# Second FFN: one subtraction per chunk of four k-tiles in place of two

## The chip, the cores and the metric

The kernel runs on one core of a Trainium2 chip. The metric is the device time of one execution in microseconds (us), the lower the better. The five engines of the core run their own instruction streams and wait for each other through semaphores: TensorE (PE in the profile, its weight loads PEld), VectorE (DVE), ScalarE (ACT), GpSimd (POOL) and SyncE (SP), which here issues the DMAs.

## The reference

One macaron layer on 256 tokens of width 2048 in float32: an FFN, a mixer of windowed attention and mLSTM, and a second FFN, each behind an RMS norm that is modulated by a condition, then a last norm. The change is in the second FFN alone:

```python
def _swiglu(x, w_in, w_out):
    a, b = jnp.split(x @ w_in, 2, axis=-1)
    return (jax.nn.silu(a) * b) @ w_out
...
u = _modulate(_rmsnorm(h, norm3_g[l]), sh3, sc3)
h = h + 0.5 * gt3 * _swiglu(u, ffn2_w_in[l], ffn2_w_out[l])
return _rmsnorm(h, final_g)
```

`w_in` is 2048 x 11264 and `w_out` 5632 x 2048.

## The kernel before

**Numbers in two parts.** TensorE multiplies in a rounded float32 format (fp32r). To keep float32's accuracy each operand is split into a rounded value `hi` and a rest `lo` = value - `hi`, and each product is three matmuls: activations' `hi` by weights' `hi` (line 862), activations' `lo` by weights' `hi` (line 866), activations' `hi` by weights' `lo` (line 870).

**Weights.** They come from memory in chunks of four k-tiles: `raw`, 128 partitions x 4 x 512 values, 1 MB, in a ring of four. A chunk is worked on in two halves, called units (`half` 0 and 1, two k-tiles each). ScalarE casts a unit's weights into `hi` (line 1445), a ring of four units, so of two chunks. VectorE subtracts and writes `lo` (line 2051 in `split`), a ring of four chunks. TensorE then does the 12 matmuls of the unit. Three semaphores count units: `hi_done` (casts), `lo_done` (rests), `unit_used` (TensorE is through). ScalarE's cast of a unit waits until TensorE is through with the unit four before it; TensorE waits for `hi_done` ahead of its first matmul of a unit and for `lo_done` ahead of the last four, those on line 870.

**The second FFN.** Its hidden width is cut into three parts of 4, 4 and 3 groups of 512 columns (`PARTS`); the phases are `ffn2_in0`, `ffn2_out0`, `ffn2_in1`, and so on. In ten groups, listed in `JOBS`, a block of 2 x 128 tokens x 4 k-tiles x 2 x 512 columns is multiplied with seven block products in place of eight (B11, T1, T2, T3, B21, T4, B22). They are the four groups of `ffn2_in1`, two groups of `ffn2_out1` (of two column blocks each), the three of `ffn2_in2` and the first of `ffn2_out2`. For them VectorE forms sums of weight blocks in float32 (`fast_sum`, lines 2296 to 2305), ScalarE casts them (line 1511), and VectorE takes their rests (`fast_rest`, line 2315). The other chunks of such a group are plain ones, 6 in nine of the groups and 4 in the last, so 12 or 8 units. They are listed by `fast_plain`, and called unit 0 to unit 11 here.

**The order on VectorE.** It is written out by hand in `fast_body` of the vector block. In a loop over the plain units it does the unit's rest, and behind certain units other work. Behind unit 3 come the rests of the last three block products and the seed of `pb`. Behind unit 5 of a part's last input group come sums of activation operands (`s_sums`), and behind unit 8 their rest (`s_rest`). Behind unit 7 comes `nat_evac`, the two rests of the hidden values of the group before (line 2280). Behind unit 9 of an output group comes `add_out` (lines 2512 and 2517). And for the next group's block products: two sums behind unit 7, one behind unit 8, one behind unit 9, and one rest behind each of units 8 to 11.

The order on TensorE is: products and units 0 and 1 interleaved, unit 2, product B22, then units 3 to 11 one behind the other. ScalarE casts a unit, then does its own side work behind the same units.

Of the kernel before, what the change touches and what calls it, by code (L numbers as in the profile page):

```python
# [26 lines left out]
F32 = mybir.dt.float32  # L27
F32R = mybir.dt.float32r
I32 = mybir.dt.int32
ALU = mybir.AluOpType  # L30
# [31 lines left out]
def build(nc, x, c, positions, w_ada, b_ada, norm1_g, ffn1_w_in, ffn1_w_out, norm2_g, w_in,  # L62
# [116 lines left out]
    def s_used(q, n):  # L179

        on_dve = sum(kt not in ON_PE[x // KD] for x in range(KD * q + n) for kt in (x % KD,))
        return on_dve, KD * q + n - on_dve
# [32 lines left out]
    with ExitStack() as ctx:  # L215
        def sb(name, shape, dt=F32):
            return ctx.enter_context(nc.sbuf_tensor(name, shape, dt))
# [4 lines left out]
        def sem(name):  # L222
            return ctx.enter_context(nc.semaphore(name))
# [11 lines left out]
        hi = sb("hi", [P, RING, 2, NC], F32R)  # L235
# [134 lines left out]
        hi_done = sem("hi_done")  # L370
        lo_done = sem("lo_done")
# [131 lines left out]
        def at_seam(ph, i, j):  # L503

            return i == 0 and j == 0 and any(ph is plan[name] for name in BEHIND)

        def slot_of(ph, i, j):

            return 0 if at_seam(ph, i, j - 1) else (ph.at(i) + j) % RING

        def raw_of(ph, i, j):

            return seam_raw[:, :, :] if at_seam(ph, i, j) else raw[:, slot_of(ph, i, j), :, :]

        def lo_of(ph, i, j):

            return seam_lo[:, :, :] if at_seam(ph, i, j) else lo[:, slot_of(ph, i, j), :, :]
# [6 lines left out]
        def hi_of(ph, i, j, half):  # L524

            if spare(ph, i, j):
                if j == 1:
                    return (hid_hi, hid_lo)[half][:, 12:16, :].rearrange("p (a k) t -> p a (k t)", a=2)
                k = 2 * (j - 2) + half
                return hi_a[:, :, :] if k == 3 else hi_b[:, k, :, :]  # L530
            return hi[:, (2 * (ph.at(i) + j) + half) % 4, :, :]
# [15 lines left out]
        def fast_plain(name, i):  # L547

            if name[5] == "i":
                return [(i, j, half, 4 + 4 * (j % 3) + 2 * half) for j in range(6) for half in (0, 1)]  # L550
            return [(b, j, half, 4 + 4 * j + 2 * half) for b in (2 * i, 2 * i + 1) for j in range(plan[name].per[b])
                    for half in (0, 1)]
# [1485 lines left out]
        def _(dve):  # L2038
# [8 lines left out]
            def split(ph, i, j, half, n, w=NC):  # L2047
                u = 2 * (ph.at(i) + j) + half
                dve.wait_ge(hi_done, u + 1)
                s = slice(2 * half, 2 * half + n)  # L2050
                dve.tensor_tensor(lo_of(ph, i, j)[:, s, 0:w], raw_of(ph, i, j)[:, s, 0:w],  # L2051
                                  hi_of(ph, i, j, half)[:, 0:n, 0:w].bitcast(F32), ALU.subtract)\
                    .then_inc(lo_done, 1)

            def start_tiles(q, kts):

                for kt in kts:
                    if kt in ON_PE[q]:
                        continue
                    k = 8 * q + kt // 2  # L2060
                    dve.wait_ge(ada_s_in[2 * (k % S_RING) + kt % 2], 16 * (k // S_RING + 1))
                    wt = ada_s[:, k % S_RING, kt % 2, :]
                    acc = ada_acc[:, q % 2, :]
                    if kt == 0:
                        if q > 1:

                            dve.wait_ge(flushed, q - 1)
                        dve.tensor_scalar(acc, wt, cond[:, 0:1], None, ALU.mult).then_inc(s_dve, 1)
                        continue
                    dve.wait_ge(s_dve, s_used(q, kt)[0])  # L2070
                    dve.scalar_tensor_tensor(out=acc, in0=wt, scalar=cond[:, kt:kt + 1], in1=acc,
                                             op0=ALU.mult, op1=ALU.add).then_inc(s_dve, 1)
# [197 lines left out]
            def turn_square(nb):  # L2270

                dve.wait_ge(nat_ok, nb + 1)
                dve.transpose(squared(nb), buf_b[:, :, :]).then_inc(nat_sq, 1)
# [9 lines left out]
            def hidden(ph, i):  # L2283

                dve.wait_ge(unit_used, 2 * (ph.at(i + 1)))
                dve.wait_ge(pa_free, ph.a0 + i + 1)
                dve.tensor_tensor(buf_b[:, :, :], buf_a[:, :, :], pb[:, :, :], ALU.mult)\
                    .then_inc(nat_ok, 1)
# [65 lines left out]
            def fast_body(name, i, mid=None, nat_last=0, hid_tail=None, gate=2):  # L2354

                ph, f = plan[name], FAST[name, i]
                inner = name[5] == "i"
                plain = fast_plain(name, i)
                last = len(plain)
                for n_, (b, j, half, k0) in enumerate(plain):  # L2360
                    split(ph, b, j, half, 2)
                    if n_ == 3:
                        if inner and i > 0:
                            hidden(ph, i - 1)
                            turn_square(ph.nat0 + i - 1)
                        elif inner:
                            mid(3)
                        elif i > 0:
                            add_out(ph, 2 * i - 1, gate)
                        elif name == "ffn2_out1":  # L2370
                            hid_tail()
                            turn_square(nat_last)
                        else:
                            hid_tail()
                            last_square(nat_last)
                        fast_rest(f, B21)
                        if name == "ffn2_out2":
                            last_blocks(PARTS[2] - 1, (0, 1))
                        fast_rest(f, T4)
                        if name == "ffn2_out2":  # L2380
                            last_blocks(PARTS[2] - 1, (2, 3))
                        fast_rest(f, B22)
                        fast_seed(f)
                        if name == "ffn2_out2":
                            nat_evac(nat_last, PARTS[2] - 1)
                    if name == "ffn2_out1" and i == 0 and n_ == 4:
                        nat_evac(nat_last, PARTS[1] - 1)
                    if inner and i > 0 and n_ == 7:
                        nat_evac(ph.nat0 + i - 1, i - 1)
                    if inner and i == ph.n - 1 and n_ == 5:  # L2390
                        s_sums(name.replace("in", "out"))
                    if inner and i == ph.n - 1 and n_ == 8:
                        s_rest(name.replace("in", "out"))
                    if not inner and n_ == last // 2 + 3:
                        add_out(ph, 2 * i, gate)
                        if name == "ffn2_out2":
                            times_final(0, None)
                    if f + 1 < len(JOBS):
                        if n_ == last - 5:
                            fast_sum(f + 1, T3)  # L2400
                            fast_sum(f + 1, T1)
                        if n_ == last - 4:
                            fast_sum(f + 1, T2)
                        if n_ == last - 3:
                            fast_sum(f + 1, T4)
                        if n_ >= last - 4:
                            fast_rest(f + 1, n_ - last + 4)
# [33 lines left out]
            def first_body(ph):  # L2441
# [17 lines left out]
                lo_unit(1)  # L2459
                start_lo(1)  # L2460
                start_tiles(1, (0,))
                lo_unit(2)
                start_tiles(1, (1,))
# [42 lines left out]
            def add_out(ph, b, gate):  # L2506

                bank, free = (pa, pa_free) if b % 2 == 0 else (pb, pb_free)
                dve.wait_ge(unit_used, 2 * (ph.at(b + 1)))
                gate_ready(gate, b)  # L2510
                row = gt_row[:, b * NC:(b + 1) * NC].unsqueeze(1).broadcast_to([P, TT, NC])
                dve.scalar_tensor_tensor(out=buf_a[:, :, :], in0=bank[:, :, :], scalar=1.0 if gate == 1 else 0.5,
                                         in1=row, op0=ALU.mult, op1=ALU.mult).then_inc(free, 1)
                use = (ph.a0 if b % 2 == 0 else ph.b0) + b // 2 + 1
                dve.wait_ge(free, use)
                hs = h[:, :, b * NC:(b + 1) * NC]
                dve.tensor_tensor(hs, hs, buf_a[:, :, :], ALU.add).then_inc(h_ok, 1)
# [282 lines left out]
            ph = plan["proj"]  # L2800
# [241 lines left out]
            ph = plan["up"]  # L3042
# [38 lines left out]
            ph = plan["ffn2_out2"]  # L3081
# [34 lines left out]
```

## Time and profile before

| | us |
|---|---|
| median of 3 runs (2061.7 to 2062.15) | 2061.86 |
| the profiled execution, its own time | 2061.43 |
| its span, first to last instruction | 2059.7 |
| TensorE busy in the span | 2037.7 (99%) |
| VectorE busy | 1716.6 (83%) |
| ScalarE busy | 1144.7 (56%) |

The mean granted TensorE clock is 0.999 of full speed. The chain of work that ended last is 96% TensorE, 2% DMA and 1% VectorE. The ten groups with seven block products stand between 1606 and 2017 us of the span, one group about every 42.3 us. Within them a 128x512 matmul starts every 0.227 us, so a unit of 12 takes 2.72 us.

### The profile page before, as it was taken

To read this page: it belongs to the slowest core of one execution; us is meant where nothing else is said; L and a number is where in the kernel's file an instruction comes from. 1 tells how busy PE (TensorE), PEld (TensorE's weight loads), DVE (VectorE), ACT (ScalarE), POOL (GpSimd) and SP (SyncE) were. 2 spreads that over 40 slices of the span, in tenths; PEclk is the share of its full clock that TensorE was granted. 3 is DMA by queue.
4 is the path that set the end of the run, shared out by engine and by line. 5 is a ranking of instruction groups with operands and counts; after the bars stand their busy time and mean duration, and the time that the engine had idled before them with its cause. 6 is when DMAs were issued, how large, how long until landed. Compare 5 with 4: busy or idle time off the path is not lost.

```text
span 2059.7 us, 24190 instructions
## 1 busy us (share of the span) xinstructions
PE 2037.7 (99%) x9235; PEld 1681.2 (82%) x9235; DVE 1716.6 (83%) x2069; ACT 1144.7 (56%) x1568; POOL 4.5 (0%) x22
## 2 busy tenths in 40 slices
PE   7999999999999999999999999999999999999998
PEld 6888888888888888888777888888888888888887
DVE  6998998888789889888877898979978677787786
ACT  4677444565345565446544676554444577755764
POOL 0000000000000000000000000000000000000000
PEclk9999999999999999999999999999999999999999
DMA  9998998998899778985555687568875655665554
GB/s 370 387 387 320 327 333 320 341 335 295 295 343 331 265 258 324 329 284 179 169 164 164 224 291 282 204 216 313 288 257 193 202 186 194 214 202 191 179 199 148
DMA packets 249571, 540.79 MB, mean 263 GB/s; under 512 B 11888, under 2 KB 14320, under 8 KB 248688
## 3 DMA queue, kind: packets, MB, share of 16 engines
q1 hardware_dynamic: 248368, 539.11, 74.3%
q8 instruction: 73, 1.20, 0.2%
q14 instruction: 42, 0.34, 0.0%
q10 hardware_dynamic: 1088, 0.15, 0.0%
HBM read 537.10 MB, written 2.11 MB: 262 GB/s over the span
## 4 chain that ended last, share of the span: by engine, by line
PE 96%; DMA 2%; DVE 1%; SPq 0%; issue 0%; ACT 0%; DVEq 0%
PE pa L862 14%; PE pb L862 14%; PE pa L870 14%; PE pb L870 14%; PE pb L866 13%; PE pa L866 13%; DMA raw<-in_ffn_w_in_dram 1%; PE pa L1015 1%; PE pa L1009 1%; PE pa L1012 1%; PE pa L1179 1%; PE pb L1170 1%; PE pb L1175 1%; PE pb L1179 1%; PE pa L1170 1%; PE pa L1175 1%
## 5 line engine op out<-in xcount | busy, mean ns | idle before, releaser
L1445 ACT CAST hi<-raw 128x1024 fp32r<-128x1024 f32 (+2 forms) x682 | 702.4, 1036 | 768.5 <-PE pb L870 355.1
L2051 DVE TENSOR_TENSOR lo<-raw,hi 128x1024 fp32r<-128x1024 f32 (+2 forms) x682 | 809.1, 1200 | 267.5 <-ACT hi L1445 264.5
L2150 DVE SCALAR_TENSOR_TENSOR ada_acc<-ada_w,cond,ada_acc 128x1024 f32<-128x1024 f32 (+1 forms) x240 | 275.0, 1146 | 6.6 <-DVE ada_acc L2150 0.5
L862 PE MATMUL pa<-hi,act_hi 128*128 128x512 f32 x840 | 231.9, 394 | 0.0
L862 PE MATMUL pb<-hi,act_hi 128*128 128x512 f32 x840 | 227.7, 393 | 0.0
L870 PE MATMUL pb<-lo,act_hi 128*128 128x512 f32 x840 | 224.6, 389 | 0.0
L870 PE MATMUL pa<-lo,act_hi 128*128 128x512 f32 x824 | 223.3, 389 | 0.0
L866 PE MATMUL pb<-hi,act_lo 128*128 128x512 f32 x824 | 220.4, 389 | 0.0
L866 PE MATMUL pa<-hi,act_lo 128*128 128x512 f32 x760 | 205.7, 389 | 0.0
L870 PEld LDWEIGHTS pb<-lo,act_hi 128*128 128x128 f32 x840 | 157.7, 188 | 32.9
L862 PEld LDWEIGHTS pb<-hi,act_hi 128*128 128x128 f32 x840 | 156.2, 188 | 33.6 <-issue 2.2
L862 PEld LDWEIGHTS pa<-hi,act_hi 128*128 128x128 f32 x840 | 155.8, 188 | 32.7 <-issue 1.3
L866 PEld LDWEIGHTS pb<-hi,act_lo 128*128 128x128 f32 x824 | 154.7, 188 | 32.4
L870 PEld LDWEIGHTS pa<-lo,act_hi 128*128 128x128 f32 x824 | 154.7, 188 | 32.3
L866 PEld LDWEIGHTS pa<-hi,act_lo 128*128 128x128 f32 x760 | 142.7, 188 | 30.1
L862 PE MATMUL pa<-hi,hid_hi 128*128 128x512 f32 x392 | 107.4, 391 | 0.0
L870 PE MATMUL pb<-lo,hid_hi 128*128 128x512 f32 (+1 forms) x388 | 106.9, 388 | 0.0
L866 PE MATMUL pa<-hi,hid_lo 128*128 128x512 f32 x392 | 106.8, 389 | 0.0
L870 PE MATMUL pa<-lo,hid_hi 128*128 128x512 f32 x392 | 106.7, 389 | 0.0
L862 PE MATMUL pb<-hi,hid_hi 128*128 128x512 f32 x346 | 93.5, 390 | 0.0
L866 PE MATMUL pb<-hi,hid_lo 128*128 128x512 f32 x346 | 93.4, 389 | 0.0
L866 PEld LDWEIGHTS pa<-hi,hid_lo 128*128 128x128 f32 x392 | 73.6, 188 | 15.4
(478 smaller groups left out, 2404.0 us busy)
## 6 DMA issues: line engine op xcount, KB each, us to landing
raw<-in_ffn_w_in_dram SPq DMA_DIRECT2D x161, 1024.0 KB, 5.3
ada_w<-in_w_ada_dram SPq DMA_DIRECT2D x224, 512.0 KB, 6.3
raw<-in_ffn_w_out_dram SPq DMA_DIRECT2D x64, 1024.0 KB, 5.1
raw<-in_w_in_dram SPq DMA_DIRECT2D x63, 1024.0 KB, 5.1
ada_s<-in_w_ada_dram SPq DMA_DIRECT2D x64, 512.0 KB, 11.6
raw<-in_ffn_w_out_dram SPq DMA_DIRECT2D x24, 768.0 KB, 4.5
raw<-in_w_out_dram SPq DMA_DIRECT2D x16, 1024.0 KB, 5.1
pair<-in_ffn_w_in_dram SPq DMA_DIRECT2D x14, 1024.0 KB, 6.9
```

The source lines that it names most:

```text
L862: pe.matmul(bank[:, tt, cols], a_hi[:, k0 + kk, tok], w_hi[:, kk, cols], start=start and kk == 0, stop=False, skip_group_check=on)
L866: pe.matmul(bank[:, tt, cols], a_lo[:, k0 + kk, tok], w_hi[:, kk, cols], start=False, stop=False, skip_group_check=on)
L870: mm = pe.matmul(bank[:, tt, cols], a_hi[:, k0 + kk, tok], w_lo[:, 2 * half + kk, cols], start=False, stop=stop and rest is None and kk == ...
L1009: pe.matmul(bank, a_hi[:, kk, :], fast_hi(o)[:, kk, :], start=start and kk == 0, stop=False, skip_group_check=True)
L1012: pe.matmul(bank, a_lo[:, kk, :], fast_hi(o)[:, kk, :], start=False, stop=False, skip_group_check=True)
L1015: mm = pe.matmul(bank, a_hi[:, kk, :], fast_lo(o)[:, kk, :], start=False, stop=kk == 1, skip_group_check=True)
L1170: pe.matmul(bank[:, tt, :], act_hi[:, k0 + kk, tok], w_hi[:, kk, 0:NC], start=q == 0 and half == 0 and kk == 0, stop=False, skip_group_che ...
L1175: pe.matmul(bank[:, tt, :], act_lo[:, k0 + kk, tok], w_hi[:, kk, 0:NC], start=False, stop=False, skip_group_check=True)
L1179: mm = pe.matmul(bank[:, tt, :], act_hi[:, k0 + kk, tok], w_lo[:, 2 * half + kk, 0:NC], start=False, stop=half == 1 and kk == 1, skip_grou ...
L1445: act.copy(hi_of(ph, i, j, half)[:, 0:n, 0:w], raw_of(ph, i, j)[:, 2 * half:2 * half + n, 0:w])\
L2051: dve.tensor_tensor(lo_of(ph, i, j)[:, s, 0:w], raw_of(ph, i, j)[:, s, 0:w], hi_of(ph, i, j, half)[:, 0:n, 0:w].bitcast(F32), ALU.subtract)\
L2150: ins = dve.scalar_tensor_tensor(out=acc, in0=wt, scalar=cond[:, kt:kt + 1], in1=acc, op0=ALU.mult, op1=ALU.add)
```

## The change

In the ten groups VectorE no longer takes the rest of a unit behind each of its two casts. It does so once per chunk, at the chunk's second unit, for all four k-tiles: it waits until both casts are done, reads both `hi` buffers (which lie side by side in the ring) and counts `lo_done` up by two.

```diff
+            def chunk_rest(ph, i, j):
+
+                c = ph.at(i) + j
+                dve.wait_ge(hi_done, 2 * c + 2)
+                rounded = hi[:, 2 * c % 4:2 * c % 4 + 2, :, :].rearrange("p a k n -> p (a k) n")
+                dve.tensor_tensor(lo_of(ph, i, j), raw_of(ph, i, j), rounded.bitcast(F32), ALU.subtract)\
+                    .then_inc(lo_done, 2)
...
                 for n_, (b, j, half, k0) in enumerate(plain):
-                    split(ph, b, j, half, 2)
+                    if half == 1:
+                        chunk_rest(ph, b, j)
                     if n_ == 3:
```

TensorE's, ScalarE's and SyncE's orders are the same as before. On VectorE 58 instructions of 128x2048 stand for 116 of 128x1024; the other 584 of line 2051 stay. Line numbers behind the new function are 8 or 9 higher.

VectorE in the last group of `ffn2_in1`, from the rests of units 6 and 7 on, before (`t` and `pair` are the next group's block sums, `s_out_lo` the rest of the operand sums):

```order
L2051 TENSOR_TENSOR lo<-raw,hi 128x1024 x2
L2280 TENSOR_TENSOR hid_lo<-hid_t,hid_hi 128x512 x2
L2296 TENSOR_TENSOR t<-pair 128x1024
L2299 TENSOR_TENSOR pair<-pair 128x1024
L2051 TENSOR_TENSOR lo<-raw,hi 128x1024
L2350 TENSOR_TENSOR s_out_lo<-s_new,s_out_hi 128x1024
L2302 TENSOR_TENSOR t<-t,pair 128x1024
L2315 TENSOR_TENSOR pair_lo<-pair,hi_b 128x1024
L2051 TENSOR_TENSOR lo<-raw,hi 128x1024
L2305 TENSOR_TENSOR t<-t,pair 128x1024
```

and the same place after:

```order
L2060 TENSOR_TENSOR lo<-raw,hi 128x2048
L2288 TENSOR_TENSOR hid_lo<-hid_t,hid_hi 128x512 x2
L2304 TENSOR_TENSOR t<-pair 128x1024
L2307 TENSOR_TENSOR pair<-pair 128x1024
L2358 TENSOR_TENSOR s_out_lo<-s_new,s_out_hi 128x1024
L2310 TENSOR_TENSOR t<-t,pair 128x1024
L2323 TENSOR_TENSOR pair_lo<-pair,hi_b 128x1024
L2060 TENSOR_TENSOR lo<-raw,hi 128x2048
L2313 TENSOR_TENSOR t<-t,pair 128x1024
```

Unit 8's rest has moved from ahead of three instructions to behind them, where it is part of the wide one with unit 9's.

VectorE in the first group of `ffn2_out1`, from the rest of unit 9 to the last before the next group, before (`buf_a` and `h` are `add_out`):

```order
L2051 TENSOR_TENSOR lo<-raw,hi 128x1024
L2512 SCALAR_TENSOR_TENSOR buf_a<-pa,gt_row 128x1024
L2517 TENSOR_TENSOR h<-h,buf_a 128x2x512
L2305 TENSOR_TENSOR t<-t,pair 128x1024
L2315 TENSOR_TENSOR pair_lo<-pair,hi_b 128x1024
L2051 TENSOR_TENSOR lo<-raw,hi 128x1024
L2315 TENSOR_TENSOR t_lo<-t,hi_b 128x1024
L2051 TENSOR_TENSOR lo<-raw,hi 128x1024
L2315 TENSOR_TENSOR t_lo<-t,hi_a 128x1024
```

and after:

```order
L2060 TENSOR_TENSOR lo<-raw,hi 128x2048
L2521 SCALAR_TENSOR_TENSOR buf_a<-pa,gt_row 128x1024
L2526 TENSOR_TENSOR h<-h,buf_a 128x2x512
L2313 TENSOR_TENSOR t<-t,pair 128x1024
L2323 TENSOR_TENSOR pair_lo<-pair,hi_b 128x1024
L2323 TENSOR_TENSOR t_lo<-t,hi_b 128x1024
L2060 TENSOR_TENSOR lo<-raw,hi 128x2048
L2323 TENSOR_TENSOR t_lo<-t,hi_a 128x1024
```

Here unit 10's rest has moved behind one block rest and joined unit 11's.

## Rows read from the trace of the kernel before

**Rows 1.** Busy us of each engine in four stretches: their sum.

```profile
sum 400.00, PE 400.00 PEld 330.12 DVE 306.37 ACT 258.26 POOL 0.00; mean PE 100.00 PEld 82.53 DVE 76.59 ACT 64.56 POOL 0.00
```

**Rows 2.** Who waited for whom, 1606 to 2003: us in total, times, longest.

```profile
DVE lo L2051 <- ACT hi L1445: 86.6, 46, 4.3
```

**Rows 3.** VectorE's instructions by form, 1500 to the end: busy us, mean ns | idle before.

```profile
L2051 DVE TENSOR_TENSOR lo<-raw,hi 128x1024 fp32r<-128x1024 f32 x160 | 194.1, 1222 | 122.3 <-ACT hi L1445 121.3
...
L2051 DVE TENSOR_TENSOR lo<-raw,hi 128x512 fp32r<-128x512 f32 x6 | 4.1, 685 | 1.0 <-ACT hi L1445 1.0
...
L2336 DVE TENSOR_TENSOR s_new<-buf_b 128x256 f32<-128x256 f32 x2 | 0.9, 426 | 0.1
```

**Rows 4.** VectorE in order of time, last group of `ffn2_in1`: start us, us.

```profile
1755.36 1.23 DVE L2051 TENSOR_TENSOR lo<-raw,hi 128x1024 fp32r<-128x1024 f32 x1 [2.82 <-ACT hi L1445]
1756.50 1.29 DVE L2280 TENSOR_TENSOR hid_lo<-hid_t,hid_hi 128x512 fp32r<-128x512 f32 x2
1757.70 1.22 DVE L2296 TENSOR_TENSOR t<-pair 128x1024 f32<-128x1024 f32 x1
1758.84 1.22 DVE L2299 TENSOR_TENSOR pair<-pair 128x1024 f32<-128x1024 f32 x1
...
1762.24 1.22 DVE L2302 TENSOR_TENSOR t<-t,pair 128x1024 f32<-128x1024 f32 x1
1763.57 1.23 DVE L2315 TENSOR_TENSOR pair_lo<-pair,hi_b 128x1024 fp32r<-128x1024 f32 x1
1764.71 1.22 DVE L2051 TENSOR_TENSOR lo<-raw,hi 128x1024 fp32r<-128x1024 f32 x1
...
1768.12 1.22 DVE L2051 TENSOR_TENSOR lo<-raw,hi 128x1024 fp32r<-128x1024 f32 x1
```

**Rows 5.** VectorE in order of time, in the tail.

```profile
2044.48 0.69 DVE L2051 TENSOR_TENSOR lo<-raw,hi_a 128x512 fp32r<-128x512 f32 x1
```

**Rows 6.** TensorE's weight loads in order of time, in the tail.

```profile
2045.22 0.19 PEld L870 LDWEIGHTS pb<-lo,hid_hi 128*128 128x128 f32 x1 [0.44 <-DVE lo L2051]
```

**Rows 7.** TensorE's matmuls in order of time, in the tail.

```profile
2044.59 0.39 PE L862 MATMUL pb<-hi_a,hid_hi 128*128 128x512 f32 x1
...
2045.56 0.64 PE L862 MATMUL pb<-hi,hid_hi 128*128 128x512 f32 x2
```

**Rows 8.** TensorE, last group of `ffn2_in1`: the `lo` matmuls of units 8 and 10.

```profile
1766.76 1.07 PE L870 MATMUL pb<-lo,act_hi 128*128 128x512 f32 x4
...
1772.20 1.07 PE L870 MATMUL pb<-lo,act_hi 128*128 128x512 f32 x4
```

**Rows 9.** ScalarE in the same group.

```profile
1763.65 1.04 ACT L1511 CAST hi_b<-t 128x1024 fp32r<-128x1024 f32 x1
```

**Rows 10.** VectorE in order of time, second group of `ffn2_out1`.

```profile
1839.95 1.23 DVE L2051 TENSOR_TENSOR lo<-raw,hi 128x1024 fp32r<-128x1024 f32 x1 [2.83 <-ACT hi L1445]
...
1848.53 1.22 DVE L2512 SCALAR_TENSOR_TENSOR buf_a<-pa,gt_row 128x1024 f32<-128x1024 f32 x1
1849.78 1.23 DVE L2517 TENSOR_TENSOR h<-h,buf_a 128x1024 f32<-128x1024 f32 x1
...
1853.19 1.22 DVE L2051 TENSOR_TENSOR lo<-raw,hi 128x1024 fp32r<-128x1024 f32 x1
```

**Rows 11.** TensorE, the same group: the `lo` matmuls of unit 10.

```profile
1856.80 1.07 PE L870 MATMUL pb<-lo,hid_hi 128*128 128x512 f32 x4
```

**Rows 12.** VectorE, second group of `ffn2_in1`: the rest of unit 7.

```profile
1670.76 1.23 DVE L2051 TENSOR_TENSOR lo<-raw,hi 128x1024 fp32r<-128x1024 f32 x1 [2.83 <-ACT hi L1445]
```

**Rows 13.** TensorE, the same group: the `lo` matmuls of unit 10.

```profile
1687.60 1.07 PE L870 MATMUL pb<-lo,act_hi 128*128 128x512 f32 x4
```

**Rows 14.** VectorE, second group of `ffn2_in1`: the seed of `pb`.

```profile
1657.14 1.22 DVE L2320 TENSOR_TENSOR pb<-q,px 128x1024 f32<-128x1024 f32 x1
```

**Rows 15.** TensorE, the same group: product B22 on `pb`.

```profile
1665.37 0.62 PE L1009 MATMUL pb<-hi_b,s_in 128*128 128x512 f32 x2
```

**Rows 16.** VectorE, first group of `ffn2_out1`: the rests of units 5 and 6.

```profile
1793.30 2.36 DVE L2051 TENSOR_TENSOR lo<-raw,hi 128x1024 fp32r<-128x1024 f32 x2 [0.18 <-ACT hi L1445]
```

## Prediction

> **What bounds the kernel now.** First the busy time by stretch: in the 400 us from 1600 to 2000, which hold nearly all of the ten groups with seven block products, TensorE is busy for 400.00 us, VectorE for 306.37, ScalarE for 258.26 [rows 1]. Nothing waits on TensorE's side; it is the bound, and a change can give time back there only by taking work from TensorE, and this one takes none. Second, the waits of that region: the largest is VectorE's, 86.6 us for ScalarE's casts [rows 2], ScalarE's for TensorE to free a buffer come next, and in none does TensorE wait for anyone. So VectorE has spare time on average. What counts is the distance, place by place, between the end of a rest (the subtraction that makes `lo`) and the matmuls that read it.
>
> **What the change removes.** The ten groups hold 6 chunks each in nine of them and 4 in the last: 58 chunks, so 116 rests of 128x1024 become 58 of 128x2048. No such wide subtraction stands in the trace. The forms there take 0.426 us (128x256), 0.685 (128x512) and 1.222 (128x1024) [rows 3]; from 512 to 1024 elements that is 1.049 ns an element, so 2048 should take 1.222 + 1.07 = 2.29 us. What follows on VectorE can start a little before an instruction's end: after a 1024-wide one 1.14 us behind its start (1757.70 to 1758.84), and after a 512-wide one 0.60 (two of them last 1.29 together, less 0.685) [rows 4]. The same slope makes that 2.20 for 2048. I take 2.29 to its end and 2.20 to the next start. Bounds: from below the elements alone at that slope with no fixed part, 2048 x 1.049 ns = 2.15 to the end and 2.06 to the next start (0.09 less, as taken above); from above two old rests laid end to end without overlap, 2 x 1.22 = 2.44 for both. The value taken is nearest to the rows, being on their line. The saving is thus 2 x 1.14 - 2.20 = 0.07 us of VectorE a chunk, 4 us over 58, all of it on an engine with idle time: nothing for the span.
>
> The Trainium skill ("VectorE: DVE Perf Modes", the section on the fixed extra latency of SBUF-source ops) gives (N+151)/0.96 ns for a float32 tensor_tensor, 1.224 us for 1024 and 2.291 for 2048, and recommends larger tiles so that the fixed part is paid once. The first figure agrees with the trace's 1.222; taken alone, its advice says gain.
>
> **What the change moves.** The rest of a chunk's first half now waits for the cast of its second half and for whatever stood before that in VectorE's order. In plain running this is harmless: a cast starts when TensorE frees a buffer, three units of 2.72 us ahead of its use. The critical stretch is the end of a group. There the unit 8 rest used to run before the sums and rests for the next group's block products; now it runs behind them, with unit 9's. The same for unit 10, behind one more rest.
>
> How late may a rest end? The trace has one place where TensorE does wait for a rest. That rest ends at 2044.48 + 0.69 = 2045.17 [rows 5], the weight load of its matmul starts at 2045.22 [rows 6]; three matmuls from 2044.59 would have reached 2045.27 at 0.227 us each, the next one starts at 2045.56 [rows 7]. The matmul concerned was due at 2045.04. A rest that ended 0.13 behind its due time cost 0.29: a rest has to end 0.16 us before its matmul is due, and TensorE loses what it ends later than that.
>
> I now lay out VectorE's order with the durations of the trace, from the rest of unit 7 on. Where the old order is replayed this way, every start comes out within 0.02 us.
>
> *Last group of `ffn2_in1` (1755 to 1773), and the like one of `ffn2_in2`.* The wide rest of units 6 and 7 starts at 1755.36 as unit 7's did, its cast being the last of the two. Behind it: +2.20 = 1757.56 two hidden rests (of the hidden values, `hid_lo`); +1.20 = 1758.76 sum; +1.14 = 1759.90 sum; +1.13 = 1761.03 the rest of the operand sums (`s_out_lo`); +1.14 = 1762.17 sum; +1.33 = 1763.50 block rest (1762.24 to 1763.57 in the trace: it waits for that sum) [rows 4]; +1.14 = 1764.64 wide rest of units 8 and 9, which ends at 1766.93. TensorE's matmuls on unit 8's `lo` are due at 1766.76 [rows 8], less 0.16: 0.33 late. Next +2.20 = 1766.84, three instructions of 1.14 to 1770.25, wide rest of units 10 and 11, end 1772.54. Due at 1772.20 [rows 8] + 0.33 - 0.16 = 1772.37: 0.17 late. Together 0.50 us. ScalarE is not delayed by the later sums: its cast of the block sum that now ends at 1762.17 + 1.22 = 1763.39 starts at 1763.65 [rows 9].
>
> *The two groups of `ffn2_out1`.* Here the order has `add_out` (two instructions, 1848.53 and 1849.78) behind unit 9's rest instead of hidden rests in front. From 1839.95: +2.20, sum, sum, sum (+1.33), block rest: wide rest at 1846.89, end 1849.18, which is in time for 1851.36 (1856.80 less 5.44). +2.20 = 1849.09, add_out 1.25 + 1.14 = 1851.48 [rows 10], three instructions of 1.14 = 1854.89, wide rest of units 10 and 11, end 1857.18. In the old order unit 10's began at 1853.19 [rows 10]. Due at 1856.80 [rows 11] - 0.16: 0.54 late. The group before it has the same order and distances and comes to 0.53.
>
> *The other six groups.* Three of them have two hidden rests behind unit 7 and no operand sums. From 1670.76 [rows 12] the same sums give wide rests that end at 1681.18 and 1686.79. Unit 10's `lo` is due at 1687.60 [rows 13]: 0.65 us to spare, and 0.82 for unit 8. The other three have more: the first group of either part has no hidden rests there, and the last of all prepares no block products.
>
> At the start of a group units 2 and 3's wide rest pushes what stands behind it back by 1.06 us (2.20 less 1.14). The last of that, the seed of `pb`, then starts at 1657.14 + 1.06 and ends at 1659.42 [rows 14]; the product on `pb` begins at 1665.37 [rows 15]. The block rests ahead of the seed are all done by 1658.3, and the first is read one third of a product (0.45), a product (1.36) and a unit (2.72) before 1665.37, at 1660.8. In the first group of `ffn2_out1` unit 5's cast comes late, and the wide rest of units 4 and 5 starts at 1793.30 as unit 5's did [rows 16]. It ends at 1795.59. Unit 4's `lo` is due six units before unit 10's, which is one group of 42.30 before 1856.80: 1814.50 - 16.32 = 1798.18, so 2.4 us to spare.
>
> **Sum.** 2 x 0.50 + 0.53 + 0.54 = 2.07 us of new stalls, nothing back. The profiled execution took 2061.43 us around its span of 2059.7; it would take 2063.5. It stands 0.4 below the median of 2061.86, so the forecast is 2061.86 + 2.0 = 2063.9 us. At the lower bound of the wide rest the same steps leave 0.03 + 0.03, twice, and 0.11, twice: 0.3 us, 2062.2. At the upper bound they grow to 0.70 + 0.41, twice, and 1.16, twice: 4.5 us, 2066.4.
>
> **Rivals.**
> *No stall at all, 2061.9.* It asks for a wide rest near its lower bound, or for TensorE to take a rest later than the tail shows. For it: the 0.16 us comes from one place alone, and 0.1 less there takes 0.6 off the sum; the late amounts, 0.17 to 0.54, are small beside the 1.22 of one instruction. Against it: six places would all have to be misjudged by up to half a microsecond, and the 1024-wide starts repeat to 0.01.
> *VectorE's saved time comes through, 2057.8.* 58 x 0.07 = 4.1 us less, if VectorE's length set the end. Against it stands that TensorE has no idle time there at all. The trace's one such wait, 0.44 us, lies in the tail behind the last of the ten groups. The Trainium skill's advice in the section named above points this way; no row does.
> *Slower by more than the noise, 2066.4.* One mechanism: the wide rest has no overlap with its neighbours and no saving, 2.44 us for each place in the queue. It decides from 2.40 on, where the sum reaches 4.1 us; the three groups with hidden rests have 0.02 us to spare at 2.44 and would stall next. For it: nothing of this width was seen. Against it: the three widths seen lie on one line.
> *The change does less than it says.* The order shows all 58 in place; no chance worth a number.
>
> **How the numbers follow.** New stalls of about 2 us: 0.62. No stall: 0.28. VectorE's saving comes through: 0.02. Past the upper bound: 0.08. A measurement of this kernel can tell about 0.2%, 4.1 us, from no change, so the first two both count as within: 0.90, faster 0.02, slower 0.08. The range reaches from the case without a stall, less the 0.25 by which the three runs differ from their middle, 2061.6, to the upper bound of the wide rest, 2066.4.
>
> **What would show it.** In the changed kernel's profile: 58 rests of 128x2048 of 2.29 us; waits of TensorE's weight load for VectorE's `lo` that were not there, at six places in four groups, 0.3 to 0.7 us each as listed (at 2045 the listing is 0.44 for a loss of 0.29); none in the other six; VectorE's busy time in the region down by about 58 x (2 x 1.22 - 2.29) = 9 us; the span up by 2. The forecast is wrong if the wide rest takes under 2.15 or over 2.44 us, if TensorE waits in the other groups as well, or if it waits nowhere.

## The result and the profile after

| | before | after |
|---|---|---|
| median of 22 runs each, us | 2061.76 (2060.67 to 2062.8) | 2064.89 (2063.2 to 2068.58) |
| the profiled execution, span | 2059.7 | 2063.1 |
| TensorE busy in the span | 2037.7 | 2039.6 |
| VectorE busy | 1716.6 | 1710.2 |

The ratio is 1.0015, with a 95% interval of 1.0010 to 1.0021, so the changed kernel is slower by 3.1 us (2.1 to 4.3). That is within 0.2%, and it is clear of zero. 2063.9 was forecast, 1.0 us below the median.

VectorE's rests by form, 1500 to the end, answer to [rows 3]:

```profile
L2060 DVE TENSOR_TENSOR lo<-raw,hi 128x2048 fp32r<-128x2048 f32 x58 | 132.8, 2289 | 102.9 <-ACT hi L1445 102.9
L2051 DVE TENSOR_TENSOR lo<-raw,hi 128x1024 fp32r<-128x1024 f32 x44 | 53.5, 1224 | 27.1 <-ACT hi L1445 26.8
```

The wide rest takes 2.289 us. The line through the narrower forms had given 2.29.

The waits from 1606 to 2008 answer to [rows 2]: who waited for whom, us in total, times, longest.

```profile
DVE lo L2060 <- ACT hi L1445: 93.7, 30, 7.3
...
PEld pb L870 <- DVE lo L2060: 3.2, 6, 0.8
...
PE pb L870 <- DVE lo L2060: 0.7, 2, 0.4
...
PEld pb L1009 <- DVE pb L2328: 0.4, 1, 0.4
```

TensorE's weight loads now wait six times for a wide rest, and once for the seed of `pb` (L2328, formerly L2320). Before, none of these seven waits was there. The sum of the four stretches of [rows 1] is now:

```profile
sum 400.00, PE 399.05 PEld 327.55 DVE 296.33 ACT 255.76 POOL 0.00; mean PE 99.76 PEld 81.89 DVE 74.08 ACT 63.94 POOL 0.00
```

VectorE is busy for 10.0 us less and TensorE idle for 0.95 more. Some 4 of these 10 us are work that the slower kernel has not reached by 2000 us; over the whole execution VectorE is busy for 6.4 us less. TensorE's idle figure understates the loss. The matmul in front of a gap counts as busy until its modelled end, so the loss is better read from the distance between starts.

VectorE in the last group of `ffn2_in1`, in order of time, answers to [rows 4]:

```profile
1755.89 2.29 DVE L2060 TENSOR_TENSOR lo<-raw,hi 128x2048 fp32r<-128x2048 f32 x1 [3.13 <-ACT hi L1445]
...
1762.71 1.22 DVE L2310 TENSOR_TENSOR t<-t,pair 128x1024 f32<-128x1024 f32 x1
1764.03 1.23 DVE L2323 TENSOR_TENSOR pair_lo<-pair,hi_b 128x1024 fp32r<-128x1024 f32 x1
1765.18 2.29 DVE L2060 TENSOR_TENSOR lo<-raw,hi 128x2048 fp32r<-128x2048 f32 x1
1767.38 1.22 DVE L2313 TENSOR_TENSOR t<-t,pair 128x1024 f32<-128x1024 f32 x1
...
1770.79 2.29 DVE L2060 TENSOR_TENSOR lo<-raw,hi 128x2048 fp32r<-128x2048 f32 x1
```

and TensorE's matmuls there, which answer to [rows 8]:

```profile
1766.32 1.07 PE L866 MATMUL pb<-hi,act_lo 128*128 128x512 f32 x4
1767.52 1.20 PE L870 MATMUL pb<-lo,act_hi 128*128 128x512 f32 x4
1768.55 1.08 PE L862 MATMUL pb<-hi,act_hi 128*128 128x512 f32 x4
...
1772.19 1.07 PE L866 MATMUL pb<-hi,act_lo 128*128 128x512 f32 x4
1773.12 1.20 PE L870 MATMUL pb<-lo,act_hi 128*128 128x512 f32 x4
1774.16 1.07 PE L862 MATMUL pb<-hi,act_hi 128*128 128x512 f32 x4
```

The wide rest of units 8 and 9 starts 9.29 us behind that of units 6 and 7, as laid out, and ends at 1767.47. The one of units 6 and 7 starts a little later than laid out. ScalarE's cast in front of it, in the kernel before:

```profile
1754.27 1.05 ACT L1445 CAST hi<-raw 128x1024 fp32r<-128x1024 f32 x1 [1.32 <-PE pa L870]
```

and after:

```profile
1754.73 1.05 ACT L1445 CAST hi<-raw 128x1024 fp32r<-128x1024 f32 x1 [1.32 <-PE pa L870]
```

The whole trace lies 0.47 us later here, so against TensorE the cast has not moved. But the narrow rest started 0.03 us behind the cast's end, and the wide one starts 0.10 behind it (from the trace's unrounded times). Behind 1500 us, all 31 wide rests that wait for a cast for over 0.3 us start after 0.10, and all 72 such narrow ones of 128x1024 in the kernel before after 0.03. These 0.07 us stood in no term of the prediction.

The eight matmuls from 1766.32 to 1768.55 should take 1.81 us and take 2.23. The eight from 1772.19 take 1.97. So this group loses 0.42 + 0.16 us. The second group of `ffn2_out1` loses most; TensorE there, answering to [rows 11]:

```profile
1857.61 1.07 PE L866 MATMUL pb<-hi,hid_lo 128*128 128x512 f32 x4
1859.03 1.20 PE L870 MATMUL pb<-lo,hid_hi 128*128 128x512 f32 x4 [0.35 <-DVE lo L2060]
1860.06 1.08 PE L862 MATMUL pb<-hi,hid_hi 128*128 128x512 f32 x4
```

and the wide rest that it waits for:

```profile
1856.69 2.28 DVE L2060 TENSOR_TENSOR lo<-raw,hi 128x2048 fp32r<-128x2048 f32 x1
```

2.45 - 1.81 = 0.64 us. By the starts of the same matmuls in both traces, the shift between 1546 and 2000 us is 2.49 us, the six places together. At the last group's seed 0.24 is added. In the tail 0.17 more is added, by a weight transfer that landed that much later. 0.47 was there already at 1546, ahead of the first changed instruction: in this profile TensorE waits 1.3 us for a transfer until 31.7 us, and its granted clock is 0.50 from 32 to 36 us, where it is 1.00 in the kernel before. Two of the profiles below have such a stretch too and lie 0.16 and 0.49 us late at 1546; the six without lie 0.1 to 0.3 early. The four add up to the 3.4 us between the spans. The change itself accounts for 2.73 of them, and that lies inside the interval of the runs (2.1 to 4.3).

### The profile page after: what moved, and what is told of

Same layout as the page of the kernel before. It is cut to its first block, busy times and chain, and to the rows that moved or that the text cites. A ratio compares the mean times of both kernels' runs of the same rounds, so it can differ in the third digit from the quotient of the medians.

```text
span 2063.1 us, 24190 instructions
## 1 busy us (share of the span) xinstructions
PE 2039.6 (99%) x9235; PEld 1681.9 (82%) x9235; DVE 1710.2 (83%) x2011; ACT 1145.4 (56%) x1568; POOL 4.6 (0%) x22
## 3 DMA queue, kind: packets, MB, share of 16 engines
HBM read 537.10 MB, written 2.11 MB: 261 GB/s over the span
## 4 chain that ended last, share of the span: by engine, by line
PE 94%; DVE 3%; DMA 1%; issue 1%; ACT 1%; ACTq 0%; DVEq 0%; SPq 0%
PE pa L862 13%; PE pa L870 13%; PE pb L870 13%; PE pb L862 13%; PE pb L866 12%; PE pa L866 12%; PE pa L1179 1%; PE pa L1170 1%; PE pb L1170 1%; PE pa L1175 1%; PE pb L1175 1%; PE pb L1179 1%; PE pa L1015 1%; PE pa L1009 1%; PE pa L1012 1%; PE pa L877 1%
## 5 line engine op out<-in xcount | busy, mean ns | idle before, releaser
L2051 DVE TENSOR_TENSOR lo<-raw,hi 128x1024 fp32r<-128x1024 f32 (+2 forms) x566 | 668.6, 1196 | 169.1 <-ACT hi L1445 166.7
L2060 DVE TENSOR_TENSOR lo<-raw,hi 128x2048 fp32r<-128x2048 f32 x58 | 132.8, 2289 | 102.9 <-ACT hi L1445 102.9
```

Of the source, the lines that this page charges most:

```text
L2060: dve.tensor_tensor(lo_of(ph, i, j), raw_of(ph, i, j), rounded.bitcast(F32), ALU.subtract)\
```

## The experiments

The theory, called Q below: the only cost is that a rest, or the seed, ends too late in VectorE's queue, and TensorE loses what that is beyond 0.16 us ahead of its matmul. The shift that each run is given is that of TensorE's matmuls against the kernel before, between 1546 us and 2000 us and at the seed of the last group. The shift decides, not the time: a ratio's interval is about 0.0009, or 1.9 us, to either side (0.0012 with 5 runs), so the times alone can barely tell the loss of 2.7 us from none. But each shift is read from one profiled execution. The tail is left out: its shift lies between -0.35 and +0.29 us over all these kernels, whatever they change.

**Wide rests where there is room.**

```diff
-                    if half == 1:
+                    late = {("ffn2_in1", 3): (4, 5), ("ffn2_in2", 2): (4, 5), ("ffn2_out1", 0): (5,), ("ffn2_out1", 1): (5,),
+                            ("ffn2_out2", 0): (1,)}.get((name, i), ())
+                    if n_ // 2 in late:
+                        split(ph, b, j, half, 2)
+                    elif half == 1:
                         chunk_rest(ph, b, j)
```

> 51 of the 58 wide rests stay; the seven chunks whose wide rest, or what stood behind it, came late in the changed kernel (chunks 4 and 5 of the last groups of ffn2_in1 and ffn2_in2, chunk 5 of both ffn2_out1 groups, chunk 1 of the ffn2_out2 group) get two narrow rests at their old places. Theory Q (the cost is only the late ends of rests in VectorE's queue): the same replay leaves at least 0.65 us to spare everywhere, so no wait of TensorE for VectorE in the ten groups and the time of before, 2061.8, ratio 1.0000. Rival W (the wide form itself costs TensorE time, by its longer turn at memory or its write-out): 51/58 of the 3.1 us stay, ratio 1.0013.

Measured: 2061.41 us (11 runs), ratio 1.0000 (0.9991 to 1.0009); shift 0.00 and 0.00. TensorE waits nowhere in the ten groups. So 51 wide rests cost nothing as such: rival W is out.

**The complement: wide rests in those seven chunks alone** (`not in` for `in` above).

> The complement: wide rests in those seven chunks alone, narrow ones in the other 51. Theory Q: a late end needs the queue that the wide rests before it have pushed back by 1.06 us. Without them the replay has the wide rests of units 8 and 9 0.75 us early, those of units 10 and 11 0.03 to 0.58 us early, so no stall there; only the last group's seed of pb is late, for 0.2 us. Time 2062.0, ratio 1.0001. Rival L (each of those places is too tight for a wide rest whatever stands before it): all of the 2.6 us of stalls stay, ratio 1.0012. Rival W: 7/58 of it, no different from Q in time, but with no wait listed.

Measured: 2062.04 us (11 runs), ratio 1.0003 (0.9993 to 1.0012). Five of the six places are without a wait, so rival L is out for them. The seed costs 0.23. But at the sixth place, unit 10 of the second `ffn2_out1` group, this profile has a larger stall than the changed kernel. TensorE's weight loads:

```profile
1855.83 0.87 PEld L866 LDWEIGHTS pb<-hi,hid_lo 128*128 128x128 f32 x4
1858.97 0.76 PEld L870 LDWEIGHTS pb<-lo,hid_hi 128*128 128x128 f32 x4 [2.27 <-DVE lo L2060]
```

and VectorE ahead of it:

```profile
1840.11 1.22 DVE L2051 TENSOR_TENSOR lo<-raw,hi 128x1024 fp32r<-128x1024 f32 x1 [2.83 <-ACT hi L1445]
1843.82 1.23 DVE L2304 TENSOR_TENSOR t<-pair 128x1024 f32<-128x1024 f32 x1 [2.48 <-DMA pair<-in_ffn_w_in_dram]
...
1856.63 2.28 DVE L2060 TENSOR_TENSOR lo<-raw,hi 128x2048 fp32r<-128x2048 f32 x1
```

VectorE stood idle for 2.48 us until a weight pair of the next group had landed, 7.5 us behind its issue. In the kernel before that transfer took 5.4 us and the idling there was 0.3. That start is 1841.52 in the trace of before, and the rests of unit 7, at 1840.11 and 1839.95, lie 0.16 apart, so the whole queue behind it was 2.14 us late. Less the 0.03 of the replay that leaves 2.11, and TensorE's shift there is 2.15.

**A second profile of the same kernel.**

> A second look at the kernel with wide rests in the seven chunks alone. In its first profile the transfer of a weight pair landed late in the second ffn2_out1 group, VectorE idled 2.5 us for it and TensorE lost 2.1 us at unit 10 behind it. Theory J (the landing varies from execution to execution): here the transfer is in time or late by another amount, and TensorE loses at most what it is late beyond the spare, 0 to 0.5 us, besides 0.2 at the last seed. Rival D (the order of this kernel delays that transfer): the same 2.5 us of idling and the same 2.1 us.

Measured: one execution, 2065.59 us. The same transfer was late again, 7.7 us behind its issue. VectorE idled 2.72 us, and TensorE's shift is 4.03 us at and behind this one place. The late transfer is what D foretold and not J; the size of the shift is neither's. Yet D does not fit all the timed runs: the lowest of the 11 took 2061.01 us, 0.5 below the median of before, and can't hold a stall of 2 us. In the eight other profiled executions, each of another kernel, this transfer took 4.9 to 5.6 us. What makes it late is left open; the profile shows instruction loading beside it in the early and in the late cases alike. That a late one turns into a stall where the spare is gone is shown twice.

Part of the 4.03 us is TensorE's clock. TensorE's matmuls behind the late rest:

```profile
1858.82 1.19 PE L870 MATMUL pb<-lo,hid_hi 128*128 128x512 f32 x4 [2.08 <-DVE lo L2060]
```

Three stretches of this second profile, with the clock in the column behind `(x0)`:

```profile
core 0: us, PE busy (x) PEld busy (x) DVE busy (x) ACT busy (x) POOL busy (x), PEclk, DMA share, GB/s
1850.00:1859.00 9.00, 6.92 (x31) 5.44 (x30) 8.97 (x8) 3.63 (x4) 0.00 (x0) 1.00 0.67 221
...
1861.00:1864.00 3.00, 3.00 (x9) 2.31 (x9) 2.30 (x3) 0.14 (x1) 0.00 (x0) 0.55 0.00 0
1864.00:1870.00 6.00, 6.00 (x28) 4.88 (x27) 4.50 (x4) 4.53 (x7) 0.00 (x0) 1.00 0.54 175
```

TensorE had been idle for 2.08 us ahead of 1858.82. The granted clock then fell to 0.55 as a mean of the stretch from 1861 to 1864, which is mostly the 1.2 GHz level, and matmuls started 0.41 to 0.43 us apart in place of 0.23. Eight such distances cost 1.6 us; the stall itself cost 2.35. In the first profile TensorE idled for 1.85 us at this place, and the clock stayed at 1.00.

**Each wide rest taken apart again, in its place.**

```diff
                     if half == 1:
-                        chunk_rest(ph, b, j)
+                        split(ph, b, j, 0, 2)
+                        split(ph, b, j, 1, 2)
```

> The changed kernel with each wide rest taken apart again: two narrow rests one behind the other at the wide one's place, behind the second unit's cast. Theory Q: the first of the two ends 1.07 us sooner than the wide one, which is more than any rest was late, while the queue is 0.07 us longer at each place; the replay has at least 0.39 us to spare at units 8 and 10 and the seed of the last group late for 0.3 us. Time 2062.1, ratio 1.0001 to 1.0002. Rival M (it is the move behind the sums and block rests that costs, not the width): the stalls of the changed kernel stay or grow, 2.6 to 2.9 us, ratio 1.0013.

Measured: 2061.81 us (11 runs), ratio 1.0003 (0.9994 to 1.0012); shift 0.00 and 0.00. The expectation had one thing wrong. `split` waits for its own unit's cast alone, so the first rest ran before the second cast was done, and the seed kept its room. The six places are as foretold: the same queue and the same order, but TensorE gets unit 8's and unit 10's `lo` one narrow rest earlier. Second group of `ffn2_out1`, VectorE:

```profile
1853.65 2.35 DVE L2051 TENSOR_TENSOR lo<-raw,hi 128x1024 fp32r<-128x1024 f32 x2
```

The first of the two starts at 1853.65 and ends 1.22 later, at 1854.87, for matmuls that start at 1856.55.

**The same, with both waiting for the second cast.**

```diff
                     if half == 1:
-                        chunk_rest(ph, b, j)
+                        dve.wait_ge(hi_done, 2 * (ph.at(b) + j) + 2)
+                        split(ph, b, j, 0, 2)
+                        split(ph, b, j, 1, 2)
```

> As the kernel with two narrow rests at the wide one's place, but the first of the two now also waits for the second unit's cast, as the wide one does; there the first waited for its own cast alone. Theory Q: still at least 0.39 us to spare at units 8 and 10; the rests in front of the last group's seed of pb are now 1.1 us later, so that one place stalls for 0.2 us. 2061.8, ratio 1.0001. Rival M (place and wait cost, not the width): 2.6 us, ratio 1.0013.

Measured: 2062.29 us (11 runs), ratio 1.0003 (0.9994 to 1.0011); shift 0.00 and 0.24. Rival M is out: order and wait together cost nothing at the six places, and 0.24 us at the seed. The rests that wait for a cast start 0.03 us behind its end here, as in the kernel before, so the 0.10 belongs to the wide form and not to waiting for the second cast. At the seed, TensorE's weight load:

```profile
2000.85 0.30 PEld L1009 LDWEIGHTS pb<-hi_b,s_out_hi 128*128 128x128 f32 x2 [0.38 <-DVE pb L2328]
```

What costs at the six places is that one instruction tells of both halves together, at its end.

**One more instruction of 1.22 us in each of nine groups, behind wide rests.**

```diff
-        sb("pad", [P, 16])
+        pad = sb("pad", [P, 16])
...
+                if o == B11 and f > 0:
+                    dve.tensor_reduce(pad[:, 0:8], ident[:, :].unsqueeze(1).broadcast_to([P, 8, P]), AX.X, ALU.max)
                 dve.tensor_tensor(fast_lo(o), fast_raw(o), fast_hi(o).bitcast(F32), ALU.subtract).then_inc(x_lo, 1)
```

> The changed kernel with one more VectorE instruction of about 1.14 us (a reduction of a constant that nobody reads) in each of nine groups, ahead of the next group's first block rest. Theory Q (TensorE loses what a rest ends later than 0.16 us ahead of its matmul): the replay gives 1.26 + 0.17 in two groups, 1.48 in two, 0.12 + 0.17 in the three groups that had no stall, 0.13 to 0.23 at the last seed: 6.8 us in all, time 2068.6, ratio 1.0033, and waits in the three groups for the first time. Rival W: VectorE has idle time for nine such instructions, nothing is added to the changed kernel, ratio 1.0015.

Measured: 2070.85 us (5 runs), ratio 1.0051 (1.0038 to 1.0063); shift 8.69 and 0.24. The three groups that had been free now wait too, first of them the second group of `ffn2_in1`. Weight loads there:

```profile
1682.93 0.76 PEld L870 LDWEIGHTS pb<-lo,act_hi 128*128 128x128 f32 x4 [0.54 <-DVE lo L2060]
...
1688.54 0.53 PEld L870 LDWEIGHTS pb<-lo,act_hi 128*128 128x128 f32 x3 [0.29 <-DVE lo L2060]
```

The pattern is as foretold, the size is not: 8.9 us in place of 6.8. I had counted 0.19 us of each new instruction as hidden in the block rest's wait for its sum. VectorE there:

```profile
1677.00 1.22 DVE L2310 TENSOR_TENSOR t<-t,pair 128x1024 f32<-128x1024 f32 x1
1678.32 1.22 DVE L2324 TENSOR_REDUCE pad<-ident 128x8 f32<-128x1024 f32 x1
1679.46 1.22 DVE L2325 TENSOR_TENSOR pair_lo<-pair,hi_b 128x1024 fp32r<-128x1024 f32 x1
```

The new one starts 1.32 behind the sum. It stands behind the wait, so it delays the rest by the full 1.14. That is 0.19 more at seven places, 1.3 us of the 2.1 that were missing. The 0.07 us by which a wide rest starts later, at the same seven, are 0.5 more; 0.3 stay open.

**The same instruction, behind narrow rests** (the kernel before with that edit).

> The kernel before with the same extra VectorE instruction of 1.22 us (a reduction that nobody reads) in nine groups, ahead of the next group's first block rest. Narrow rests everywhere. The instruction cost the changed kernel 6.2 us on top of its own loss. Theory Q: with narrow rests the least spare in the nine groups is 2.24 us, so 1.1 us is left behind the extra instruction and TensorE waits nowhere; 2061.6, ratio 1.0000. Rival V (VectorE's or a memory's load as such slows TensorE): some of the 6.2 us show here too, ratio up to 1.003.

Measured: 2061.72 us (11 runs), ratio 1.0001 (0.9992 to 1.0009); shift 0.00 and 0.00. One instruction costs 6.2 us on nine places or nothing, by whether the spare of 2.2 us and more has been spent. Rival V is out.

**Wide rests with the block rests behind them.**

```diff
-                    if half == 1:
+                    if name == "ffn2_out2" and n_ < 4:
+                        split(ph, b, j, half, 2)
+                    elif half == 1:
                         chunk_rest(ph, b, j)
...
-                        if n_ >= last - 4:
-                            fast_rest(f + 1, n_ - last + 4)
+                        for o in {last - 3: (B11,), last - 2: (T1,), last - 1: (T2, T3)}.get(n_, ()):
+                            fast_rest(f + 1, o)
```

> The changed kernel with wide rests kept (56 of 58; the first two chunks of the ffn2_out2 group get narrow ones), and in its place the order changed: the next group's block rests B11 and T2 move from ahead of the wide rests of units 8 and 9, and 10 and 11, to behind them. Theory Q: the replay has at least 0.79 us to spare at every rest and the seed as before, so no wait; 2061.6, ratio 1.0000 (0.9995 to 1.0005). Rival G (the saved VectorE time, 4 us, comes through once the stalls are gone): 2057.6, ratio 0.998. Rival W (wide form): ratio 1.0013.

Measured: 2061.57 us (11 runs), ratio 1.0001 (0.9992 to 1.0010); shift 0.00 and 0.00. The last group of `ffn2_in1` there, VectorE:

```profile
1762.13 1.22 DVE L2310 TENSOR_TENSOR t<-t,pair 128x1024 f32<-128x1024 f32 x1
1763.27 2.28 DVE L2060 TENSOR_TENSOR lo<-raw,hi 128x2048 fp32r<-128x2048 f32 x1
...
1768.88 2.28 DVE L2060 TENSOR_TENSOR lo<-raw,hi 128x2048 fp32r<-128x2048 f32 x1
```

The wide rests end at 1765.55 and 1771.16, some 1 us ahead of their matmuls. This keeps 56 of the 58 wide rests and loses nothing. It gains nothing either, so rival G is out: the time of VectorE that they save goes into its waits for ScalarE. No version here beats the kernel before. In the ten groups none can that leaves TensorE's work as it is, because TensorE is never idle there in the kernel before. The wait in the tail, which costs up to 0.3 us, is left, and these runs could not tell so little.

## Why the prediction was right

- *TensorE is the bound and VectorE's saving is worth nothing.* Right: between 1546 and 2000 us TensorE's starts lie at the places of before with 0, 51 and 56 wide rests, and with 58 they lie as far apart as before everywhere but at the six stalls.
- *The wide rest takes 2.29 us to its end and 2.20 to the next start.* Right: 2.289, and 1765.18 to 1767.38. VectorE's busy time was to fall by 9 us; over the whole execution it falls by 6.4. The 9 came from adding up whole durations, although an instruction's last 0.09 us can overlap the next one.
- *Which places are late.* All six foretold were, and none of the others among the rests. In the six other groups TensorE waits for no rest, as foretold. The listed waits are 0.3 to 0.8 us; 0.3 to 0.7 was forecast.
- *How much.* 0.42 + 0.16, twice, and about 0.64, twice, against 0.33 + 0.17 and 0.54: the shift is 2.49 us and 2.07 had been summed. The rule of 0.16 us holds: in the second `ffn2_out1` group the wide rest ended at 1856.69 + 2.28 = 1858.97, the matmul was due at 1857.61 + 0.91 = 1858.52, and 0.45 + 0.16 = 0.61 of the 0.64 follow. The term that was too small is where the queue begins. Each layout let the wide rest of units 6 and 7 start where unit 7's narrow one did, and it starts 0.07 us later behind the same cast. From there on the layout holds: 9.29 us against 9.28 in the last group of `ffn2_in1`. In four groups this makes 0.28 of the 0.42 us that the sum fell short; the rest is some hundredths at each place.
- *The pushed-back seed of `pb` has room.* Wrong for one group of ten, by 0.24 us. The prediction had named a wait of TensorE in a group other than the four as a sign of being wrong, and this is one, though for the seed and not for a rest. The room was read from the second group of `ffn2_in1` ([rows 14, 15]: 5.9 us) and taken for all. In the last group, `ffn2_out2`, VectorE also does eight block transposes between those rests. Its seed in the kernel before,

```profile
1998.73 1.22 DVE L2320 TENSOR_TENSOR pb<-q,px 128x1024 f32<-128x1024 f32 x1
```

ends at 1999.95, and TensorE's product on `pb` there starts soon behind it:

```profile
2001.03 0.63 PE L1009 MATMUL pb<-hi_b,s_out_hi 128*128 128x512 f32 x2
```

That left 1.08 us. The wide rest takes 1.06 of them, a wait begins 0.16 ahead, and the wide rest starts 0.07 late: 0.21 of the 0.24 us. The most crowded group should have been the one looked at.
- *The rivals.* No stall, saving comes through and past the upper bound: none of them. The range 2061.6 to 2066.4 holds the median. Of the 1.0 us above the forecast, the trace accounts for 0.42 and 0.24; what is left is within the interval of the runs.
- *The spread, of which the prediction said nothing.* Single executions of the changed kernel reach 2068.6, above the range, and they are spread wider (2063.2 to 2068.6, against 2060.7 to 2062.8). Part of this goes with TensorE's clock. The record lists the mean granted clock of each execution. In six of the 22 it is 0.999, and they took 2063.20 to 2065.04, median 2064.20. In six it is 0.997, and they took 2064.81 to 2068.58. The kernel before, in the 27 executions run beside the first experiments, has fifteen at 0.999, median 2061.46, and two at 0.997. So at 0.999 the change costs 2.7 us, which is what the trace gives. Where in the slower executions the clock was low, and whether the new stalls brought it down, is not known: in the one that was profiled it was low at 32 to 36 us, long before the change. A late transfer that becomes TensorE's loss, as it did twice in another kernel, would widen the spread as well. That is argued and not shown.

## What to carry to other kernels

Joining two instructions saves a fixed part once, but their consumer gets the first half only when both are done, and the first half waits for the second's input. With the bound engine full, only that second effect is left: before joining, lay out the queue of the engine at the place where it is most crowded, and compare each end with the time when the reader is due. If the join is wanted anyway, move work whose reader is far away from ahead of it to behind it; spare time on a queue also absorbs late transfers, and with the spare gone a transfer that landed 2 us late twice became a stall of 2 us and more.

## What the runs showed of the hardware

- A float32 subtraction on VectorE takes 0.685, 1.22 and 2.289 us for 512, 1024 and 2048 elements a partition, and the next instruction may start 0.09 us before its end. Behind one of 1024 elements the next starts after 1.14 us, and after 1.32 if it stands behind a wait for that one's result (1677.00 to 1678.32).
- A rest of 128x2048 that waits for ScalarE's cast starts 0.10 us behind the cast's end, one of 128x1024 starts 0.03 behind it (31 and 72 places, the same in every kernel here).
- A rest that ends less than 0.16 us ahead of its matmul's due time delays TensorE by the difference. The weight load starts 0.05 us behind the rest's end and its matmul starts with it; the matmul after that one starts 0.34 us later in place of 0.23. The distances behind it are 0.23 again. So 0.05 + 0.11 make up the 0.16.
- Four idle stretches of TensorE of 1.25 to 1.47 us (with the extra instruction) and one of 1.85 us left the granted clock at 1.00. Another, of 2.08 us, was followed by a stretch at the 1.2 GHz level, in which eight matmuls started 0.41 to 0.43 us apart.
